# First attention by heads: V's product as three fp32r products over two query tiles, transposes in two groups a unit

## The reference

```
s = (jnp.einsum('bqhd,bkhd->bhqk', qn, k_nope, preferred_element_type=jnp.float32)
     + jnp.einsum('bqhr,bkr->bhqk', qr, k_rope, preferred_element_type=jnp.float32))
p = jax.nn.softmax(s * scale, axis=-1).astype(v.dtype)
return jnp.einsum('bhqk,bkhd->bqhd', p, v)
```

## Time and profile before

| | |
|---|---|
| three runs, median | 4364.99 us (4360.97 to 4367.25) |
| the profiled execution | 4367.83 us, of it 4366.0 from the first to the last instruction |
| TensorE busy over the span | 4022.8 us (92%) |
| VectorE, ScalarE, POOL busy | 2973.9, 2433.6, 1231.3 us |
| granted TensorE clock, mean | 0.959 |
| this stage, from its first DMA to the next stage's first product | 497.94 to 1187.80 us, 690 us |

### The profile page before, as it was taken

How to read it: one execution, slowest core, us unless ns; L and a number is a source line. 1 busy time by engine, 2 the same in 40 slices (tenths; PEclk the granted TensorE clock), 3 DMA queues, 4 the chain that set the end, 5 groups by cost and what they waited for, 6 DMA issues and landing times. The chain is left out here.

```text
span 4366.0 us, 61138 instructions
## 1 busy us (share of the span) xinstructions
PE 4022.8 (92%) x21445; PEld 3412.4 (78%) x21445; DVE 2973.9 (68%) x3831; ACT 2433.6 (56%) x3867; POOL 1231.3 (28%) x846
## 2 busy tenths in 40 slices
PE   8989799999897997999799999997698799999995
PEld 8978689888776876888678888886687588888872
DVE  6667555555486884444477777774655799999985
ACT  6733333333323554333388888887422577777773
POOL 0000145445300110000288888884000111111114
PEclk9999899999998998999899999998899799999998
DMA  6666733333496433222440000004543688888987
GB/s 230 219 212 235 230 113 110 104 118 111 145 287 195 138 105 124 67 67 67 106 163 15 15 23 15 15 10 150 195 155 111 227 319 318 316 321 326 377 318 303
DMA packets 417337, 728.63 MB, mean 167 GB/s; under 512 B 121744, under 2 KB 314384, under 8 KB 396304
## 3 DMA queue, kind: packets, MB, share of 16 engines
q1 hardware_dynamic: 382560, 642.02, 43.0%
q10 hardware_dynamic: 20640, 50.87, 3.3%
q0 software_dynamic: 13968, 33.58, 2.0%
HBM read 601.84 MB, written 213.91 MB: 187 GB/s over the span
## 5 line engine op out<-in xcount | busy, mean ns | idle before, releaser
L2675 POOL TENSOR_TENSOR a_PL<-a_PT,a_PH 128x512 fp32r<-128x512 f32 x512 | 674.4, 1332 | 133.5 <-ACT a_PH L2794 130.3
L2844 DVE TENSOR_REDUCE a_part<-a_pA 128x1 f32<-128x1024 f32 (+1 forms) x384 | 360.0, 955 | 95.4 <-PE a_pA L2698 90.9
L2792 ACT ACTIVATE a_PT<-a_pB 128x512 f32<-128x512 f32 x576 | 340.7, 592 | 78.6 <-PE a_pB L2721 77.3
L2794 ACT ACTIVATE a_PH<-a_PT 128x512 fp32r<-128x512 f32 x576 | 364.4, 633 | 18.4
L3478 POOL DMA_INDIRECT w_XG<-between_h,all_slots x65 | 120.8, 1858 | 779.0 <-PE e_pT L3760 724.8
L1397 ACT ACTIVATE a_PT<-a_pT 128x512 f32<-128x512 f32 x128 | 69.5, 594 | 409.0 <-PE a_pT L1327 409.0
L1432 DVE TENSOR_REDUCE a_maxima<-a_pS 128x1 f32<-128x512 f32 x256 | 176.0, 689 | 132.6 <-PE a_pS L1309 131.1
L1341 PE MATMUL a_pO<-a_V,a_PT 128*128 128x128 f32 x2048 | 249.4, 275 | 1.0 <-DVE a_PT L1445 1.0
L1341 PEld LDWEIGHTS a_pO<-a_V,a_PT 128*128 128x128 f32 x2048 | 243.4, 192 | 6.5 <-DVE a_PT L1445 1.2
L1239 POOL TENSOR_TENSOR a_QL<-a_RQ,a_QT 128x512 fp32r<-128x512 f32 x16 | 20.5, 1284 | 800.6 <-DVE a_QP L1467 800.6
L2739 PE MATMUL a_pO<-a_PL,a_VH 128*128 128x512 f32 x576 | 225.7, 392 | 3.1 <-DVE a_PL L2854 2.1
(11 more groups left out here) (651 smaller groups left out, 10617.5 us busy)
## 6 DMA issues: line engine op xcount, KB each, us to landing
w_gate<-in_moe_w_gate SPq DMA_DIRECT2D x47, 2048.0 KB, 7.7
w_up<-in_moe_w_up SPq DMA_DIRECT2D x47, 2048.0 KB, 12.4
w_down<-in_moe_w_down SPq DMA_DIRECT2D x46, 2048.0 KB
between_yb<-e_Y ACTq DMA_DIRECT2D x46, 512.0 KB, 7.0
a_row_w<-in_w_ada SPq DMA_DIRECT2D x16, 1024.0 KB, 5.5
between_x<-m_X SPq DMA_DIRECT2D x32, 512.0 KB, 2.8
between_yb<-a_zeros SPq DMA_DIRECT2D x32, 512.0 KB, 14.6
between_tv<-pz_OV SPq DMA_DIRECT2D x16, 576.0 KB, 2.9
```

Source lines behind the costliest of these rows:

```text
L2675: pool.tensor_tensor(PL[:, t % RING, :], PT[:, t % RING, :], PH[:, t % RING, :].bitcast(F32), ALU.subtract).then_inc(S["p_low"], 1)
L2792: act.activation(PT[:, t % RING, :], pB[t % 2][:], ACT.Exp, scale=scale).then_inc(S["p_ready"], 1)
L2794: act.activation(PH[:, t % RING, :], PT[:, t % RING, :], ACT.Copy).then_inc(S["p_high"], 1)
L2844: dve.tensor_reduce(part[:, h, r % (NG2 // G4):r % (NG2 // G4) + 1], src, AX_X, ALU.max).then_inc(S["maxed"], 1)
```

## The change

Only this stage is rewritten, under the name attention_1; attention is gone. Loops are written out instead of run as hardware loops.

- The order of units: head by head, 16 query tiles each. Only the keys and V of two heads are held, and a later head's are loaded and split while the one before runs. The rope keys have tiles of their own (KRH, KRL).
- Query tiles go in pairs q of two units. Queries are loaded, split and stored by pairs; the outputs wait for four units.
- V and the exps are split into high and low parts in fp32r. For each key tile, V is now the stationary operand: V high times both the high and the low exps of two query tiles (512 columns), V low times the high exps (256 columns). The output comes out transposed; ScalarE copies one half, VectorE adds the other (gather_output), and TensorE transposes it back (back), once a unit.
- ScalarE copies all four transposed groups, which rounds them to the high part, and VectorE subtracts, for the low part.
- The order on TensorE: scores 0 and 1, transposes of groups 0 and 1, scores 2 and 3, transposes of groups 2 and 3 of the unit before; V's products of a pair stand in four parts, two at the end of the pair's following even unit and two inside the odd one.
- The piece of the mixing weight (load_split) is fetched a unit of this side work ahead, and the scan's first tables are loaded when the third head is done.

```diff
+        KRH, KRL = k.sb("KRH", [P, SEQ], F32R), k.sb("KRL", [P, SEQ], F32R)
+        KH, KL = ([M["keys_1"][m], k.sb(name, [P, SEQ], F32R)[:]] for m, name in enumerate(("KH", "KL")))
+        VH, VL = ([k.sb(f"{name}{b}", [P, NT, DV], F32R) for b in range(2)] for name in ("VH", "VL"))
+        RQ, QT = k.sb("RQ", [P, 2, PW]), k.sb("QT", [P, 2, PW])
+        QP, QH, QL = ([k.sb(f"{n}{b}", [P, PW], F32R) for b in range(2)] for n in ("QP", "QH", "QL"))
+        PR = [k.sb(f"PR{b}", [P, SEQ]) for b in range(2)]
+        PT = k.sb("PT", [P, NT, 2, PW], F32R)
+        OT = k.sb("OT", [P, PW])
+        OB = [k.sb(f"OB{b}", [P, 2, DV]) for b in range(2)]
+        top, bias, total = ([k.sb(f"{n}{b}", [P, 1]) for b in range(2)] for n in ("top", "bias", "total"))
+        HELD = 8
+        inverse = k.sb("inverse", [P, HELD])
...
+        def turned(u, g):
+            return u * GROUPS + g + 1
+
+        def highs_ready(h):
+            return 1 + 2 * h
...
+            def load_piece(i):
+                src = I["w_ada"].rearrange("(k p) n -> p k n", p=P)[:, :, ds(i * P, P)]
                 sp.dma_start(ada_w[:], src).then_inc(S["ada_loaded"], 16)
...
+            def pair(q):
+                if q + 2 < PAIRS:
+                    wait(S["q_split"], q + 2)
+                    load_query(q + 2)
+                if q >= 3:
+                    store(q - 3)
+
+            def quarter(i):
+                if i >= 2:
+                    store_row(i - 2)
+                load_row(i)
+                h = i // 4
+                if i % 4 == 1 and 1 <= h < H1 - 1:
+                    wait(S["p_ready"], GROUPS * NT * h)
+                    load_keys(h + 1)
+                    wait(S["o_ps"], PER_HEAD * h)
+                    load_values(h + 1)
+                pair(2 * i)
+                if i + 1 < QUARTERS:
+                    wait(S["ada_multiplied"], i + 1)
+                    load_piece(i + 1)
+                for name in ("w_in_2", "w_out"):
+                    part = ds(i * (DM // NT), DM // NT)
+                    sp.dma_start(D[name][part, :], I[name][part, :]).then_inc(S["copied"], 16)
+                if i:
+                    store_split(i - 1)
+                    load_split(i)
+                pair(2 * i + 1)
 
             def load_scan():
-                wait(S["p_ready"], ((NT - 1) * heads + 1) * banks)
+                wait(S["p_ready"], GROUPS * NT * (H1 - 1))
...
-            tiles(sp, NT, tile, last=3)
-            load_scan()
-            store(tile_at(NT - 1))
-            store_row(tile_at(NT - 1))
-            store_split(tile_at(NT - 1))
-            sp.wait_ge(S["split2_stored"], 32 * NT)
-            sp.wait_ge(S["row_stored"], 16 + 16 * NT)
+            load_query(0)
+            sp.dma_start(KRL[:].bitcast(F32), D["kr"]).then_inc(S["kr_loaded"], 16)
+            load_keys(0)
+            for dst, name in ((cc, "c2"), (b_col, "b_ada_col"), (g1, "g1")):
+                sp.dma_start(dst[:], I[name]).then_inc(S["c_loaded"], 16)
+            load_values(0)
+            sp.wait_ge(S["q_split"], 1)
+            load_query(1)
+            load_piece(0)
+            load_keys(1)
+            load_values(1)
+            load_split(0)
+            for i in range(QUARTERS):
+                quarter(i)
...
+            def low_values(h):
+                pool.wait_ge(S["v_high"], highs_ready(h))
+                low = VL[h % 2][:].rearrange("p n d -> p (n d)")
+                pool.tensor_tensor(low, low.bitcast(F32), VH[h % 2][:].rearrange("p n d -> p (n d)").bitcast(F32), ALU.subtract).then_inc(S["v_split"], 1)
...
+            for i in range(QUARTERS):
+                h = i // 4 + 1
+                low_queries(2 * i + 1)
+                if i % 4 == 3 and h < H1:
+                    low_values(h)
+                modulation(i)
+                if i + 1 < QUARTERS:
+                    low_queries(2 * i + 2)
+                row(i)
+                if i % 4 == 2 and h < H1:
+                    low_keys(h)
 
         @block.tensor
...
+            def scores(u, g):
+                q, h = u // 2, u // NT
+                if g == 0 and u % 2 == 0:
+                    pe.wait_ge(S["q_split"], q + 1)
+                if g == 0 and u % NT == 0:
...
                 mm.then_inc(S["s_ps"], 1)
 
-            def moved(u, g):
-                if g in act_moves:
-                    pe.wait_ge(S["act_moved"], u * len(act_moves) + act_moves.index(g) + 1)
...
+            def turn(u, g):
+                pe.wait_ge(S["p_ready"], turned(u, g))
+                if turned(u, g) > 2:
+                    pe.wait_ge(S["moved"], turned(u, g) - 2)
+                for j in range(4):
...
+            def apply(q, g):
+                h = q // PER_HEAD
+                pe.wait_ge(S["moved"], turned(2 * q + 1, g))
+                if g == 0 and q % PER_HEAD == 0:
+                    pe.wait_ge(S["v_split"], h + 1)
+                if g == 0 and q:
+                    pe.wait_ge(S["o_turned"], q)
+                def rests(j):
+                    return pe.matmul(pO[:, 0:PW], VL[h % 2][:, j, :], PT[:, j, 0, :], start=False, stop=False)
+
+                for j in range(4 * g, 4 * g + 4):
+                    if j:
+                        rests(j)
+                    mm = pe.matmul(pO[:], VH[h % 2][:, j, :], PT[:, j].rearrange("p a b -> p (a b)"), start=j == 0, stop=j == NT - 1)
+                    if j == 0:
+                        rests(j)
+                if g == GROUPS - 1:
+                    mm.then_inc(S["o_ps"], 1)
+
+            def back(u):
+                pe.wait_ge(S["o_turned"], u // 2 + 1)
+                if u:
                     pe.wait_ge(S["o_ready"], u)
-                for j in range(groups[g][1]):
-                    jj = 4 * g + j
-                    mm = pe.matmul(pO[:, 0:dv], PT[:, jj, :], values(V, h, jj), start=jj == 0, stop=jj == key_tiles - 1)
-                if g == banks - 1:
-                    mm.then_inc(S["o_ps"], 1)
...
+            def slot(u):
+                q, second = u // 2, u % 2
+                here, turns, applies = u < UNITS, 1 <= u <= UNITS, 2 <= u < UNITS + 2
+                if here:
+                    scores(u, 0)
+                    scores(u, 1)
+                if second and applies:
+                    apply(q - 1, 2)
+                if turns:
+                    turn(u - 1, 0)
+                    turn(u - 1, 1)
+                if u >= 4:
+                    back(u - 4)
+                if here:
+                    scores(u, 2)
+                    scores(u, 3)
+                if second and applies:
+                    apply(q - 1, 3)
+                if turns:
+                    turn(u - 1, 2)
+                    turn(u - 1, 3)
+                if not second and applies:
+                    apply(q - 1, 0)
+                    apply(q - 1, 1)
+
+            for u in range(UNITS):
+                slot(u)
+                if u >= 4 and u % 4 == 1:
+                    modulation(u // 4 - 1)
+                if u >= 4 and u % 4 == 3:
+                    row(u // 4 - 1)
+            for u in range(UNITS, UNITS + 4):
+                slot(u)
+                if u == UNITS + 1:
+                    modulation(QUARTERS - 1)
+            row(QUARTERS - 1)
 
         @block.scalar
         def _(act):
-            def move(t, h):
-                u = unit(t, h)
-                for g in act_moves:
...
+            def move(u, g):
+                act.wait_ge(S["t_ps"], turned(u, g))
+                act.activation(PT[:, 4 * g:4 * g + 4, 0, queries(u)], pT[g % 2][:].rearrange("p (a b) -> p a b", b=P), ACT.Copy).then_inc(S["high_moved"], 1)
+
+            def exp(u, g):
+                b = u % 2
+                if g == 0:
+                    act.wait_ge(S["bias_ready"], u + 1)
+                    if u >= 2:
+                        act.wait_ge(S["t_ps"], turned(u - 2, GROUPS - 1))
+                act.activation(PR[b][:, g * BANK:(g + 1) * BANK], pS[:, g, :], ACT.Exp, bias=bias[b][:], scale=scale,
+                               accum_out=sums[b][:, g:g + 1]).then_inc(S["p_ready"], 1)
+
...
+            def copy_output(q):
+                act.wait_ge(S["o_ps"], q + 1)
+                if q:
+                    act.wait_ge(S["o_back"], 2 * q)
+                act.activation(OT[:], pO[:, 0:PW], ACT.Copy).then_inc(S["o_copied"], 1)
+
+            def slot(u):
+                if u % 2 == 0 and u >= 4:
+                    copy_output(u // 2 - 2)
+                if 1 <= u <= UNITS:
+                    move(u - 1, 0)
+                    move(u - 1, 1)
+                    move(u - 1, 2)
+                if u < UNITS:
+                    exp(u, 0)
+                    exp(u, 1)
+                if 1 <= u <= UNITS:
+                    move(u - 1, 3)
+                if u < UNITS:
+                    exp(u, 2)
+                    exp(u, 3)
+
+            high_keys(0, 0, 1)
+            high_values(0, 0, 1)
             act.wait_ge(S["c_loaded"], 48)
```

(121 more changed lines are left out.)

414 lines of the change are left out of this document (151 added, 263 removed).

## The result

The changed kernel takes 4381.33 us (median of 7 runs, 4372.27 to 4386.95), the kernel before on the same chip 4362.82 (7 runs): ratio 1.0036 [1.0026, 1.0047]. On two later occasions the ratios were 1.0042 [1.0027, 1.0056] and 1.0036 [1.0024, 1.0048]. So it is slower, by some 16 us by the ratio (the medians of that occasion lie 18.5 apart). The range (4343 to 4386) holds the time; the forecast (4361, most likely no change or faster) had the sign wrong.

A forecast was written before the change was run, and what follows sets the result against it. The prediction took TensorE, busy throughout at full clock, as the bound. Waits +2, start -8, end +6 and leaving the block -4 made -4 us, from the runs' median 4365.0 to 4361; 8-in-10 range 4343 to 4386.

The forecast's parts named there:

- TensorE's work: V's product in each unit: 2.80 us against 3.57, unit's work 9.30 us, 0.66 less.
- Rival (5): V's product gets no shorter, a 256-column product taking 0.22 us: 49 us more, 4410; chance 0.02.
- The waits: New TensorE pauses from ScalarE's and VectorE's order give back the 0.66 a unit: four units 40.8 us against 40.7, taken as +2.
- The wait for exp: Before the next unit's scores after an odd unit, TensorE stands 1.09 us, once a pair, since the third bank's copy precedes exp.
- the one for the gathering: Before the transpose back, TensorE waits for VectorE's gathered output: 0.06 us, but 1.3 in every fourth unit, behind the gate row.
- Rival (2): The waits don't bite, ScalarE reaching exp in time: four units 38.1 us, total 4320; chance 0.08.
- Start and end: Stage's edges: first scores 1.6 us earlier, unit 4 reached 8 us earlier, end +6, leaving the block -4.
- The step that failed: POOL's splits of a later head's keys and values, a quarter of a head ahead, were to cost nothing.
- Rival (4): VectorE steps cost 0.05 to 0.1 more while POOL works; 15 groups lose 1 us each: 4376; chance 0.11.
- rival (3): The 1.09 pauses lower TensorE's clock, 1.7 us lost each time: 4388 with 16 falls, 4415 in every pair; chance 0.10.
- The other stages keep their code: Rest of the program outside this stage: code unchanged, no term in the sum.
- the tie that I forecast: Whole kernel: no measurable change, within about 0.2% or 8.7 us, was given 0.44, faster 0.31, slower 0.25.

The follow-up runs named there:

- both experiments on it: Two edits of the changed kernel: exp ahead of the third copy in odd units, ratio 1.0001; gate row's last two steps at the unit's end, 1.0002.
- the third trace: The changed kernel, unedited, traced on the last of its three occasions: stage 705.5 us, ratio to the kernel before 1.0036.
- the gate row's steps moved: Changed kernel with only the gate row's first step ahead of gathering the output, the other two at the unit's end: ratio 1.0002 to the kernel before.
- the pieces: Changed kernel with GpSimd's splits of keys and V cut in eight: ratios 1.0039, then 1.0014 to the kernel before; with both reorderings 0.9934.
- the later split: VectorE's weight-piece split at units 11, 27 and 43 done a unit later, GpSimd's splits whole; on the changed kernel with both reorderings: ratio 0.9928.
- both reorderings: Changed kernel with exp ahead of the third copy in odd units and the gate row's last two steps at the unit's end: ratio 0.9969.
- the doubled split: Changed kernel with GpSimd's key split done twice, one behind the other: stage 714.6 us, whole time 4421 in one run, not comparable.
- the split moved: Changed kernel with VectorE's weight-piece split at units 11, 27 and 43 done a unit later: ratio 1.0007 to the kernel before, stage 691.7 us.

## Why the prediction was right or wrong

**TensorE's work: right.** V's pair of products takes 0.35 us, as the earlier trace rows gave:

```profile
701.00 0.40 PE L1348 MATMUL a_pO<-a_PT,a_VH 128*128 128x512 f32 x1
701.24 0.28 PE L1343 MATMUL a_pO<-a_PT,a_VL 128*128 128x256 f32 x1
701.35 0.40 PE L1348 MATMUL a_pO<-a_PT,a_VH 128*128 128x512 f32 x1
```

Rival (5) is out.

**The waits: right.** An odd unit was to take 9.30 + 1.09 = 10.39 and takes 10.42 to 10.44; an even one 9.36 and takes 9.46; with the gate row 10.6 and takes 10.54. The gain of 0.66 a unit was given back, and both experiments on it found the waits where the order in the diff had put them. The wait for exp reads 0.58 or 0.67 us, as the little products of 0.43 at the end of the odd unit fill the rest of the 1.09; the one for the gathering is 0.87, where I had put 1.3. Rival (2) is out.

**Start and end: right in sum.** First scores -1.7 (-1.6); to unit 4 37.3 us (39.3; 38.9 in the third trace, with the fall of the clock in unit 1). From unit 63 to the end of the gate row 28.2 us (27), from there to the next stage 2.3 (3.5).

**The step that failed** is "POOL's splits of a later head's keys and values (2048 columns each) lie a quarter of a head ahead ... nothing". I asked only when their results are wanted, not what else runs while they do. In place of nothing it cost 14.7 us in three units: VectorE's copy of 0.42 us was held to 3.72 beside GpSimd's 4.58, and TensorE stood 2.89 behind it. The kernel before could have told me: I took its pause of 2.19 for the clock alone and didn't ask what had caused it, which was such a hold. Part of that is the clock: with the gate row's steps moved, the two such units without a fall take 12.64, 3.0 more than their like, against 3.8 to 5.8 more here. A smaller omission lies in the same stretch: in units 10, 26 and 42 (10.26 instead of 9.46) ScalarE's copy of half of the later head's keys, 1.09 us, stands ahead of the output's copy by the trace, 0.8 x 3 = 2.4 us (no run tests it); and four units are 0.16 longer, 2.4 more over the stretch. Less 1.1 for unit 4, which has no gate row yet, these make 18.4 of the 18.2.

**Rival (4)** named the right engines (VectorE can't hold its order while POOL works) and even the right price, +15, but that is luck, since it was by another mechanism: steps dearer by 0.05 to 0.1 in all units with gate row. Nothing of that shows: the maxima take 0.68 and the subtraction from PSUM 0.69, beside GpSimd's pieces too. What was held in these traces had all its operands in SBUF, and it was held for the rest of GpSimd's instruction. That the range holds the measured time is luck too: its upper end came from this rival and from part of rival (3), not from the step that failed.

**Rival (3), the clock.** In the plain stretch the pauses, 0.58 to 0.87 us each, left it at 1.00 (window 650 to 690 above), as the 1.28 in the earlier trace rows had said. By the rule of the Trainium skill ("TensorE: Matmul & The Clock Gate", A second HAM failure mode) it would have swung there; the trace doesn't agree. At the unforeseen 2.9 it fell each time, nine times in the three traces of this kernel.

**"The other stages keep their code"** is true and didn't make them equal. The median of the changed kernel lies 16 us above, the stage explains 10 to 12. In five of the seven kernels with an edit (the pieces and the later split with both reorderings are the others) the whole time also stands 5 to 7 us higher than the stage says. By the traces the mixing stage is 1 to 5 us shorter, while the experts' stage takes 844.5 and 843.5 in the kernel before and 844.5 to 855.4 (mean 848.5) in eleven traces of changed ones (without the doubled split), and from its last product to the last stage's first it is 24.4 and 24.5 against 25.7 to 27.9. Why stages that differ in nothing should be longer, or whether that is the spread of eleven traces, stays open; no run here isolates it. With the split moved, even so, the change is the tie that I forecast: 1.0007.

## What to carry over

When work on GpSimd is moved into a steady loop, list what VectorE does from SBUF to SBUF in the same microseconds: such an instruction can be held until GpSimd's ends, and everything queued behind it with it. The profile shows that as a long duration of the held instruction, not as a wait, so compare the longest with the median of each line. Move the one off the other, or cut GpSimd's instruction short. And a wait multiplied by its count is the most that its removal can give: subtract first what stands in its shadow.

## What was unexpected of the hardware

- The hold is all or nothing. A copy of 0.42 us took 3.72, a subtraction of 0.69 took 4.87. They end 0.28 and 0.55 us behind GpSimd's instruction, and the 128x1280 subtraction of the kernel before (1.48 alone, 4.62 there) 1.35 behind it: each time 0.13 or 0.14 less than it takes alone, so nearly all of its own time comes after that end. Nor is a small one spared: the silu's last step, 16 columns, took 3.04 us at the stage's start, beside the split of V (timeline of the changed kernel):

```profile
510.30 4.56 POOL L1261 TENSOR_TENSOR a_VL<-a_VL,a_VH 128x2048 fp32r<-128x2048 f32 x1 [4.21 <-ACT a_VH L1439]
...
511.85 3.04 DVE L1583 SCALAR_TENSOR_TENSOR all_cs<-a_half_c,a_cc 128x16 f32<-128x16 f32 x1 [3.10 <-ACT a_half_c L1466]
```

- Not every VectorE instruction with its operands in SBUF is held. The reduction of a unit's four sums and the reciprocal (L1501, L1503) took 0.15 and 0.16 us beside GpSimd's split as anywhere else (the reciprocal is in the timeline of unit 12 above).
- GpSimd is held too, where VectorE comes first. Its 128x768 split of the rope keys, begun 0.12 us behind a VectorE subtraction of 1.49 us, took 3.04 us in the changed kernel; such splits took 1.83 to 1.85 in the kernel before where they ran by themselves or beside VectorE's reads of PSUM.
- The same pause doesn't always cost the clock. With the gate row's steps moved, TensorE stood 2.89 us at the same three places. Behind the first the window reads

```profile
636.50:639.90 3.40, 3.39 (x19) 2.74 (x20) 3.31 (x8) 0.60 (x1) 0.00 (x0) 1.00 0.03 7
```

and the three units took 12.64, 12.64 and 15.21: the granted clock fell at the third alone, and the fall cost 2.6 us. In the kernel with pieces a pause of 1.54 took it down at two of three places (13.06 against 11.50: 1.6 us).
